# Paged caches in transfers of three head pairs, one buffer for local caches, and half of the paged keys issued by ScalarE

## The reference

```python
for g, (win, dil) in enumerate(DSA_PAIRS):          # local: 3 groups of 2 heads, caches of 128, 256, 256 tokens
    o, lse, nbuf = dsa_group_sample(qb[..g..], kb[..g..], vb[..g..], bufs_in[g], bias_b[..g..], win, dil)
yb = dsa_combine(outs, lses)
yc = moba_sample(qc, kc, vc, gather_pages(pool_k, page_table), gather_pages(pool_v, page_table), bias_c)

def gather_pages(pool, page_table):                 # pool: 20 pages of 128 tokens x 6 heads x 64
    g = pool[page_table]                            # 8 sequences x 2 pages
    return g.reshape(g.shape[0], g.shape[1] * g.shape[2], g.shape[3], g.shape[4])
```

## Time and profile before

| | value |
|---|---|
| median of three runs | 962.34 us |
| time of the profiled run | 963.47 us |
| its span | 961.6 us |
| TensorE busy | 939.1 us (98%), 7413 products |
| VectorE busy | 619.1 us (64%) |
| ScalarE busy | 414.4 us (43%) |
| GpSimd busy | 74.7 us (8%) |
| DMA | 104.57 MB, mean 109 GB/s |
| TensorE's granted clock | digit 9 (90% or more of full speed) in all 40 slices |

### The profile page before, as it was taken

The page is one execution under the profiler, slowest core; times in us unless marked ns, Lnnn a source line. Parts: engine busy times, 40 slices in busy tenths (PEclk is TensorE's granted clock), DMA queues, the critical chain, the costliest instruction groups (busy, mean ns, idle before and its releaser), DMA issues.

```text
span 961.6 us, 18735 instructions
## 1 busy us (share of the span) xinstructions
PE 939.1 (98%) x7413; PEld 915.6 (95%) x7413; DVE 619.1 (64%) x1203; ACT 414.4 (43%) x782; POOL 74.7 (8%) x106
## 2 busy tenths in 40 slices
PE   8999999999999899899999999999999999999998
PEld 7999989999988899899999999999999999999997
DVE  5835556444787464453537678899657998458863
ACT  7433233444544342322222455566325555226553
POOL 1100023011210200020203000000000000000000
PEclk9999999999999999999999999999999999999999
DMA  7683326432211667222222243422322324213212
GB/s 239 159 259 58 47 80 101 159 111 69 88 49 44 155 180 217 80 89 89 88 89 88 89 154 151 175 88 90 131 89 66 111 88 132 88 45 103 85 34 94
DMA packets 103874, 104.57 MB, mean 109 GB/s; under 512 B 10090, under 2 KB 100712, under 8 KB 103452
## 3 DMA queue, kind: packets, MB, share of 16 engines
q1 hardware_dynamic: 100040, 92.22, 31.8%
q0 software_dynamic: 3552, 11.08, 4.0%
q10 hardware_dynamic: 196, 0.08, 0.0%
HBM read 97.51 MB, written 15.45 MB: 117 GB/s over the span
## 4 chain that ended last, share of the span: by engine, by line
PE 85%; DMA 4%; DVE 4%; SPq 3%; ACT 2%; issue 2%; POOL 0%; DVEq 0%; ACTq 0%; POOLq 0%
PE acc L1383 38%; PE acc L669 34%; SPq L901 2%; DMA G<-gd 2%; PE acc L1288 1%; PE acc L1409 1%; PE acc L1264 1%; DMA ring<-in_cache_dsa_kv 1%; PE acc L1142 1%; PE acc L1131 1%; PE acc L1248 1%; ACT h_hi L1933 1%; PE acc L1102 1%; PE acc L1469 1%; PE acc L1342 1%
## 5 line engine op out<-in xcount | busy, mean ns | idle before, releaser
L669 PE MATMUL acc<-h_hi,w_hi 128*128 128x288 f32 (+1 forms) x816 | 256.9, 315 | 1.9 <-DVE h_lo L2700 1.2
L669 PE MATMUL acc<-h_lo,w_hi 128*128 128x288 f32 (+1 forms) x816 | 234.8, 288 | 0.0
L669 PE MATMUL acc<-h_hi,w_lo 128*128 128x288 f32 (+1 forms) x800 | 229.9, 287 | 0.0
L669 PEld LDWEIGHTS acc<-h_hi,w_hi 128*128 128x128 f32 x816 | 153.8, 188 | 10.1 <-issue 4.6
L669 PEld LDWEIGHTS acc<-h_lo,w_hi 128*128 128x128 f32 x816 | 154.0, 189 | 4.1 <-issue 2.4
L669 PEld LDWEIGHTS acc<-h_hi,w_lo 128*128 128x128 f32 x800 | 150.5, 188 | 0.0
L644 ACT ACTIVATE w_hi<-raw 128x1024 fp32r<-128x1024 f32 x66 | 70.0, 1060 | 180.2 <-PE acc L669 180.2
L1383 PE MATMUL acc<-h_hi,w_hi 128*128 128x272 f32 x412 | 119.5, 290 | 0.6
L1383 PE MATMUL acc<-h_hi,w_lo 128*128 128x272 f32 x412 | 119.0, 289 | 0.0
L1383 PE MATMUL acc<-h_lo,w_hi 128*128 128x272 f32 x412 | 118.9, 289 | 0.0
L652 DVE TENSOR_TENSOR w_lo<-raw,w_hi 128x1024 fp32r<-128x1024 f32 x66 | 82.8, 1254 | 20.4 <-ACT w_hi L644 18.1
(11 more groups left out here) (405 smaller groups left out, 2044.1 us busy)
## 6 DMA issues: line engine op xcount, KB each, us to landing
raw<-in_w_in SPq DMA_DIRECT2D x25, 1024.0 KB, 5.3
raw<-in_w_gate_up SPq DMA_DIRECT2D x22, 1024.0 KB, 5.1
raw<-in_w_down SPq DMA_DIRECT2D x8, 1024.0 KB, 5.3
rev<-tab POOLq DMA_DIRECT2D x1, 4352.0 KB, 22.1
ring<-in_cache_dsa_kv SPq DMA_DIRECT2D x4, 1024.0 KB, 7.7
raw<-in_w_out SPq DMA_DIRECT2D x4, 1024.0 KB, 5.2
out<-in_cache_dsa_kv SPq DMA_DIRECT2D x2, 2016.0 KB
ring<-in_cache_moba_k SPq DMA_DIRECT2D x48, 64.0 KB, 2.2
```

Source lines behind the costliest of these rows:

```text
L669: ins = nc.tensor.matmul(acc[:, bank, 0:HALF[half]], a[:, k, :], two(b[:, kx + k, :], half), start=first and k == k0 and c == 0, stop=last ...
```

## The change

The paged caches get one buffer `paged` for three pairs, in the place of the first three ring buffers, and a page now comes with all three pairs in one transfer (128 rows, three pieces of 512 bytes each in SBUF, 1536 bytes in one piece in memory). The local caches use one buffer `window`, in the place of the fourth (pair 2's values use a third of `paged`). The pair order becomes 0, 3, 4, 1, 5, 2 and the order of the value parts follows. Keys of pages 0 to 7 are issued by SyncE, those of pages 8 to 15 by ScalarE, which reads these page numbers itself between blocks 12.5 and 19.5. Paged keys are waited for in four groups of four pages, with one semaphore each.

```diff
-        ring = [Map(a_v)("ring0", [P, 16, P]), Map(a_v + 8192)("ring1", [P, 16, P]),
-                Map(a_v + 16384)("ring2", [P, 16, P]), Map(a_s)("ring3", [P, 16, P])]
+        paged = Map(a_v)("paged", [P, 3, 16, P])
+        window = Map(a_s)("window", [P, 16, P])
...
-        Q_ORDER = (1, 3, 0, 4, 2, 5)
-        V_ORDER = (3, 0, 1, 4, 2, 5)
-        pv = [(3, 0), (0, 0), (3, 1), (1, 0), (4, 0), (1, 1), (4, 1), (2, 0), (5, 0), (2, 1), (5, 1)]
+        Q_ORDER = (0, 3, 4, 1, 5, 2)
+        pv = [(3, 0), (3, 1), (1, 0), (1, 1), (4, 0), (4, 1), (2, 0), (2, 1), (5, 0), (5, 1), (0, 0)]
...
+        window_order = [("k", 0), ("k", 1), ("k", 2), ("v", 1), ("v", 0)]
+        pages_in = [sem(f"pages_in{i}") for i in range(4)]
+        def cache_ready(pe, what, q, tile):
+            if (what, q) == ("v", 2):
+                pe.wait_ge(pages_in[0], 128 + 16)
+            elif q < 3:
+                pe.wait_ge(window_in, 16 * (window_order.index((what, q)) + 1))
+            elif what == "k":
+                pe.wait_ge(pages_in[tile // 4], 64)
+            else:
+                for done in pages_in:
+                    pe.wait_ge(done, 128)
...
+                    def page_load(m, cache, done):
+                        src = cache[0, bass.ds(pages[m], 1)].rearrange("o p h d -> p (o h d)")
+                        sp.dma_start(paged[:, :, m, :], src.rearrange("p (q n) -> p q n", n=P)).then_inc(done, 16)
+                    yield T_SA + 0.38
+                    sp.wait_ge(sem("pt_tr"), ND + len(segs))
+                    window_load("k", 0, window_in)
+                    yield T_SA + 0.4
+                    sp.wait_ge(sem("o_mm"), ND + len(segs))
+                    sp.wait_ge(sem("new4"), 2)
+                    sp.wait_ge(sem("v_stored"), 32 * 6)
+                    for m in range(8):
+                        page_load(m, I["cache_moba_k"], pages_in[m // 4])
+                    yield T_SA + 1.35
+                    sp.wait_ge(sem("kt_tr"), k_ends[0])
+                    window_load("k", 1, window_in)
+                    yield T_SA + T_QK + (k_ends[3] - 1) * D_QK
+                    sp.wait_ge(sem("kt_tr"), k_ends[3])
+                    window_load("k", 2, window_in)
+                    yield T_SA + T_QK + (k_ends[4] - 1) * D_QK
+                    sp.wait_ge(sem("kt_tr"), k_ends[4])
+                    for m in range(16):
+                        page_load(m, I["cache_moba_v"], pages_in[m // 4])
+                    yield T_SA + T_QK + (k_ends[5] - 1) * D_QK
+                    sp.wait_ge(sem("kt_tr"), k_ends[5])
+                    window_load("v", 1, window_in)
+                    yield T_SA + T_P + 0.08 + 2 * D_PV
+                    sp.wait_ge(sem("pv_mm"), pv.index((3, 1)) + 1)
+                    window_load("v", 2, pages_in[0])
+                    yield T_SA + T_P + 0.08 + 4 * D_PV
+                    sp.wait_ge(sem("pv_mm"), pv.index((1, 1)) + 1)
+                    window_load("v", 0, window_in)
...
+                def late_pages():
+                    numbers = []
+                    for m in range(8, 16):
+                        yield 4.5 + m
+                        numbers.append(act.value_load(I["page_table"][m // 2:m // 2 + 1, m % 2:m % 2 + 1], min_val=0, max_val=19))
+                    yield unit_time(NU + 2, 0.3)
+                    act.wait_ge(sem("o_mm"), ND + len(segs))
+                    act.wait_ge(sem("new4"), 2)
+                    act.wait_ge(sem("v_stored"), 32 * 6)
+                    for m in range(8, 16):
+                        src = I["cache_moba_k"][0, bass.ds(numbers[m - 8], 1)].rearrange("o p h d -> p (o h d)")
+                        act.dma_start(paged[:, :, m, :], src.rearrange("p (q n) -> p q n", n=P)).then_inc(pages_in[m // 4], 16)
```

## The result

The changed kernel takes **969.12 us** (966.97 to 971.85, six runs) against 962.62 us (961.69 to 964.34, six runs) of the kernel before: a ratio of 1.0062, with 95% certainty between 1.0050 and 1.0073. The forecast was 961.1 us with a range of 957.8 to 964.3: the kernel became slower by 6.5 us where a gain of 1.2 us was forecast, and the time lies 4.8 us outside the range. Each experiment's ratio is against executions of the kernel before that belong to it; their medians lie between 962.33 and 963.72 us, so ratios are compared and not times. The profiled execution of the changed kernel took 968.46 us, its span is 966.6 us (before: 963.47 and 961.6), so it shows 5.0 of the 6.5 us.

The account below looks back on a forecast made before the run. TensorE, busy 98% of the span, was taken as the bound, so only its waits could change: 6.54 us gone, 5.3 us new, net -1.2 us off the 962.34 us median, giving 961.1 us, range 957.8 to 964.3.

Parts of the forecast that it names:

- The waits that the edit was to remove, 6.54 us: TensorE's waits before first key tiles (1.79), step 4 (1.25), step 14 (1.92) and last paged values (1.58 us).
- steps 10 and 18: Key steps, numbered 0 to 21, that first use local caches of pairs 1 and 2; no wait was forecast at either.
- two queues side by side bring page 7 together with page 15: SyncE's and ScalarE's key pages: served alike, page 7 lands when everything has landed, taken as 331.8.
- its bounds: Issue time of a joined three-pair page transfer: between 0.53 us and 1.6 us, taken as 0.53.
- the reads: ScalarE's eight reads of page numbers, blocks 12.5 to 19.5: 0 to 1 us on the path, taken as 0.
- the landing of page 7: Last page of SyncE's key queue, wanted by step 3: 4.04 MB through the DMA engines, landing at 331.8.
- TensorE's clock: Read as at its upper level, 2.4 GHz, in all 40 slices; no term for it in the sum.
- -1.2: Net forecast of the whole edit in us: 6.54 of waits gone, 5.3 of new wait.
- Cost nothing while the pages are the later ones: ScalarE's eight issues hold the new scores' copy, step 0 up to 3.7 us late; no cost, otherwise 1 to 4.7 us.
- The term of 5.3 us for step 3: Key step 3, free at 326.5, waits for pages 4 to 7 until 331.8: 5.3 us.
- A little for the slowest engine: Small allowance within the 331.8 landing time of the key pages, beside bias rows in about half the phase.
- C: Rival, key stage: ScalarE held until 331.5, step 3 at 336.1, +3.1 us, 965.4 us; chance 0.09.

Follow-up runs that it names:

- experiment 7: The changed kernel with even key pages issued by SyncE and odd ones by ScalarE: 965.72 us, ratio 1.0023.
- Experiment 1: The changed kernel with all sixteen key pages issued by SyncE; ScalarE issues none and reads no page numbers: 960.94 us, ratio 0.9985.
- experiment 4: The changed kernel without ScalarE's reads of page numbers, loading other pages of the same size: 967.26 us, ratio 1.0040.
- experiment 2: The kernel before with only the eight reads of page numbers on ScalarE added: 965.36 us, ratio 1.0029.
- experiment 6: Idle products fill TensorE's key-stage waits: changed kernel 976.33, with fewer 969.10 us; last, on the changed kernel without reads, 965.05 us against 967.26 unfilled.
- experiment 9: SyncE-only changed kernel with key steps later and closer: 960.54 us, ratio 0.9970; also with GpSimd's bias rows held back until step 3 is turned: 962.92 us, 0.9998.
- experiment 5: The kernel before with four pauses of TensorE, of different lengths, among the feed-forward products: 976.32 us, one execution.
- experiment 8: The SyncE-only changed kernel with three one-pair transfers for each page instead of one joined transfer: 988.44 us, one execution.
- experiment 3: The changed kernel with ScalarE's reads of page numbers earlier, at blocks 12.5 to 16.0: 973.03 us, ratio 1.0104.

## Why the prediction was wrong

**What held.** The waits that the edit was to remove, 6.54 us, are gone, and the local caches need no more room than one buffer: no wait at steps 10 and 18 or for values. The DMA rate was right (279 GB/s from 318.8 to 335.7, 277 to 295 assumed), and so was the assumption that two queues side by side bring page 7 together with page 15: by 335.7, when page 7 was in, ScalarE's queue had moved all but 0.01 MB of its 1.57 (and experiment 7). The joined issue takes 0.79 us (12.63 / 16), between its bounds. Experiment 1, the edit without ScalarE's half, lies at 960.94. That it is so near the forecast is in part luck: it has four waits of 4.6 us in all where the sum has one of 5.3.

**What failed, in short.** Three terms: the reads (taken as 0, measured 2.1 to 2.8 us), the landing of page 7 (2.7 us too early), and TensorE's clock (not in the sum, 2.3 us). Added to -1.2 they give 5.9 to 6.6 us, and 6.5 was measured. Each alone would have left the time inside the range.

**The reads, taken as 0 with 1 us as the upper end.** They cost 2.1 us (experiment 4) to 2.8 us (experiment 2); in the profiled execution 1.3 us. The nearest row, an idle time of about 2 us beside one of them, says nothing of the length of a read, beside which ScalarE stands up to 6.8 us here; and I looked at the slack beside one of the eight, not at the tightest. A bound taken from what surrounds an operation is no bound on the operation.

**"Cost nothing while the pages are the later ones."** ScalarE was free at 326.65; forecast was 324.0 to 326.3, with the later start of the stage (1.3 us) 325.3 to 327.6, so the size was right, and that wait ends before the pages, as reckoned. But it is a wait of 3.03 us, and behind it TensorE works at 1.2 GHz until 330.4. By the clock column that is 0.24 x 2 + 0.50 x 2 + 0.11 x 2 = 1.7 us of work, which the page wait behind it still hid.

**The term of 5.3 us for step 3.** Step 3 was to be free at 326.5; with the 1.3 us by which the stage now starts later that is 327.8, and it came at 335.81: 8.0 us, 2.7 more. The sum let 4.04 MB pass before page 7; by 335.7 the engines had moved 4.71 MB. The other 0.7 MB are the weight load behind the pages: SyncE's queue had moved 2.77 MB by then, and its local cache and eight pages are 2.10. "A little for the slowest engine" was 0.3 us and should have been over 2. How the weight load got past the last page is not shown.

**The clock, nowhere in the sum.** I wrote that the clock is at its upper level in all 40 slices and then let it stay there. But the kernel before had no wait in this stage above 1.92 us, and the edit made two above 3. Behind the 3.64 us wait the column gives 0.50 x 4 + 0.17 x 2 = 2.3 us of work lost, and nothing hides it; experiment 6 measures 2.2 us, experiment 9 2.3 us.

**The sum once more, in the profiled executions.** Forecast for the stage: -1.2. Later pages +2.7, clock behind them +2.3, a third fall of the clock at 405 to 409 worth 1.7, less the wait of 1.5 us before L669 that it swallows, +0.2: together +4.0, against +3.7 read from the last turned probabilities, where the first local load can go, to the end (649.3 us instead of 645.6). That the third fall comes from the edit isn't shown: experiment 5, with the instructions of the kernel before, has one at 399. With the reads' 1.3 us that is the 5.0 us of the span. The medians lie 1.5 us further apart than the two profiled executions; the reads are larger there (2.1 to 2.8), which may be most of it; no run shows the rest.

**The rivals.** C named the right engine and the right direction, at half the size (3.1 of 6.5 us), but by another mechanism: it had ScalarE's release decide step 3. It did not; the pages did, and the long waits lowered the clock. That the edit is slower had 0.08, and the range had no case in which waits of the same sum cost different amounts.

By the Trainium skill ("DMA: Bandwidth & Descriptors", Issuing engines are not separate DMA queues) issuing from several engines saves only the sequencer's time, which is usually small. The trace agrees on the first half: from 326 to 334 the changed kernel's windows show 261 to 296 GB/s with two queues, those of experiment 1 276 to 291 with one. The trace also shows that the saved time is not free elsewhere: SyncE's issuing fell from 12.63 to 7.06 us, and ScalarE's compute queue paid 7.32.

## What to carry to other kernels

Don't price waits of TensorE by their sum alone: here three waits of 0.71, 0.86 and 2.24 us cost 2.3 us less than two of 0.38 and 3.40 that add up to the same. A wait of 3 us or more nearly always brought the lower clock here, and with it about 1.7 to 2.3 us more; but the length alone didn't decide it, so put such a loss into the range with a chance and don't expect it for certain. Before you issue transfers or read registers on an engine that computes, look up which of its results is wanted next, and reckon the issues (here 0.91 us each) and the reads (up to 6.8 us) as time in which that result stands. If a load is split over two queues, deal the pieces out in the order of their use.

## What the runs showed of the hardware that was not expected

- TensorE's clock has the two levels that the Trainium skill names ("TensorE: Matmul & The Clock Gate", Part 1), and the rows agree: 0.50 or 1.00, with a value between only in windows that hold a change. Behind waits of 3 us and more it fell in eight of nine cases (3.03 twice, 3.08, 3.12, 3.40, 3.49, 3.64, 4.10) and stayed in one (3.34, experiment 7). Between 2 and 3 us it fell behind 2.03, 2.31 and 2.86 and stayed behind 2.15, 2.24, 2.62 and 2.90. So no length found here parts the two. The waits of experiment 4 (2.26 and 2.80 us with 1.4 us between) and the row of long ones in experiment 8 are not in this count.
- The clock also fell where TensorE had hardly waited: at 126.3 in experiment 7, and between 399 and 408 behind a wait of 0.39 us in five of the fourteen profiled executions (the changed kernel, experiments 3, 4 and 5, and the filled kernel at the end of experiment 6, with the clock at 1.00 through the key stage). Experiment 5 has the instructions of the kernel before there, and the kernel before has no fall. What brings these falls is open.
- Beside one read of four bytes into a register ScalarE was idle for 3.3 us (experiment 3), 4.5 (the changed kernel), 6.1 (experiment 2) and 6.8 us (experiment 7, before the copy at 171.57).
- Eight transfers of 192 KB took ScalarE 7.32 us and SyncE 7.06 us side by side, sixteen took SyncE 12.63 us alone. Each of the joined issues takes 0.8 to 0.9 us either way.
- A product of two constant 128 x 128 operands in f32 took 0.23 us and stands in the trace as two instructions (26 for 13 products, 3.06 us); a turned tile in the same format is one instruction and takes 0.15 (0.60 us for four, with their overlap).
